# Five transpose groups per head pair, one-column row sums and turned keys in a two-block transformer kernel

## The reference, cut to what matters

```python
mod_l = jax.nn.silu(c) @ w_mod[l] + b_mod[l]          # modulation: rows of 512 columns at a time in the kernel
k = blockdiag(x_c, w_kblk)                            # mLSTM keys; the kernel wants them in both layouts
...
def one_block(qi):                                    # later layers, 128 queries at a time
    sc = jnp.einsum('bqkgd,bskd->bkgqs', qi, k_all, preferred_element_type=jnp.float32)
    p = jax.nn.softmax(sc, axis=-1).astype(v_all.dtype)
    return jnp.einsum('bkgqs,bskd->bqkgd', p, v_all)
```

## Time and profile before

| what | value |
|---|---|
| median of 3 runs | 3628.36 us (3626.59 to 3631.72) |
| the profiled execution | 3626.34 us |
| span of its instructions | 3624.6 us |
| mean granted TensorE clock | 0.948 |
| PE busy | 3266.9 us, 90% of the span |
| PEld busy | 2622.5 us, 72% |
| DVE busy | 1872.3 us, 52% |
| ACT busy | 1415.7 us, 39% |
| POOL busy | 694.9 us, 19% |

### The profile page before, as it was taken

One profiled execution on the slowest core, in us unless ns is written; L12 is line 12 of the kernel. 1 busy time (PEld: TensorE's weight loads), 2 busy tenths in 40 slices (PEclk: granted clock), 3 DMA queues, 4 the chain that ended last, 5 costly groups with the idle time before them and its releaser, 6 DMA issues. The chain is left out here.

```text
span 3624.6 us, 43080 instructions
## 1 busy us (share of the span) xinstructions
PE 3266.9 (90%) x17137; PEld 2622.5 (72%) x17137; DVE 1872.3 (52%) x2593; ACT 1415.7 (39%) x1941; POOL 694.9 (19%) x460
## 2 busy tenths in 40 slices
PE   7989998999999799794999999599988896998879
PEld 3767775778777687673788887588877675886757
DVE  4356775444444344646788888424415443152543
ACT  4222232333333244431777777431126334212640
POOL 2100001011111155300454554320010003000000
PEclk7999999999999899896999999799989997999999
DMA  6326555101000131324999999411121134112112
GB/s 197 113 96 199 168 173 175 33 25 43 26 25 25 50 116 64 129 88 166 350 382 390 379 389 374 137 60 54 38 60 24 47 111 156 57 44 57 30 70 82
DMA packets 248690, 471.51 MB, mean 130 GB/s; under 512 B 25455, under 2 KB 137072, under 8 KB 248492
## 3 DMA queue, kind: packets, MB, share of 16 engines
q1 hardware_dynamic: 232904, 410.88, 32.7%
q0 software_dynamic: 15264, 57.70, 4.8%
q10 hardware_dynamic: 324, 0.15, 0.0%
HBM read 406.12 MB, written 55.22 MB: 127 GB/s over the span
## 5 line engine op out<-in xcount | busy, mean ns | idle before, releaser
L2525 DVE TENSOR_TENSOR exp_wl<-wts_raw,exp_wh 128x2048 fp32r<-128x2048 f32 x144 | 393.9, 2771 | 106.2 <-ACT exp_wh L2485 106.2
L2485 ACT ACTIVATE exp_wh<-wts_raw 128x2048 fp32r<-128x2048 f32 x192 | 368.4, 1921 | 196.1 <-PE exp_gate L2414 64.1
L2691 PE MATMUL pr_ps<-l_h_high,pr_wh 128*128 128x512 f32 (+1 forms) x896 | 335.5, 374 | 0.0
L2692 PE MATMUL pr_ps<-l_h_low,pr_wh 128*128 128x512 f32 (+1 forms) x896 | 329.9, 368 | 0.0
L2693 PE MATMUL pr_ps<-l_h_high,pr_wl 128*128 128x512 f32 (+1 forms) x896 | 329.2, 367 | 0.0
L2384 POOL TENSOR_TENSOR exp_wl<-wts_raw,exp_wh 128x2048 fp32r<-128x2048 f32 x48 | 229.1, 4773 | 265.2 <-ACT exp_wh L2485 265.2
L842 PE MATMUL in_ps<-iw_h_high,in_wh 128*128 128x512 f32 (+1 forms) x696 | 273.2, 393 | 0.0
L843 PE MATMUL in_ps<-iw_h_low,in_wh 128*128 128x512 f32 (+1 forms) x696 | 263.4, 378 | 0.0
L844 PE MATMUL in_ps<-iw_h_high,in_wl 128*128 128x512 f32 (+1 forms) x696 | 263.0, 378 | 0.0
L2853 DVE TENSOR_TENSOR pr_wl<-pw_raw,pr_wh 128x512 fp32r<-128x512 f32 x84 | 57.8, 692 | 334.2 <-ACT pr_wh L2771 332.9
L2691 PEld LDWEIGHTS pr_ps<-l_h_high,pr_wh 128*128 128x128 f32 x896 | 170.3, 190 | 30.5 <-issue 2.4
(11 more groups left out here) (510 smaller groups left out, 7343.5 us busy)
## 6 DMA issues: line engine op xcount, KB each, us to landing
wts_raw<-in_w_e_gate SPq DMA_DIRECT2D x64, 1024.0 KB, 9.6
wts_raw<-in_w_e_up SPq DMA_DIRECT2D x64, 1024.0 KB, 8.8
wts_raw<-in_w_e_down SPq DMA_DIRECT2D x64, 1024.0 KB, 7.6
g_scratch<-in_w_mod SPq DMA_DIRECT2D x80, 512.0 KB, 4.5
pw_raw<-in_w_in SPq DMA_DIRECT2D x88, 256.0 KB, 2.9
iw_raw<-in_w_in SPq DMA_DIRECT2D x74, 256.0 KB, 4.6
mod_w<-in_w_mod SPq DMA_DIRECT2D x4, 2048.0 KB, 11.9
wo_w<-in_w_out SPq DMA_DIRECT2D x2, 4096.0 KB, 13.3
```

What stands on the lines that cost most here:

```text
L2485: act.activation(wh[:, m % RING], raw[:, m % RAW_RING], ACT.Copy).then_inc(high, 1)
L2525: dve.tensor_tensor(wl[:, m % RING], raw[:, m % RAW_RING], wh[:, m % RING].bitcast(F32), ALU.subtract).then_inc(low, 1)
L2691: nc.tensor.matmul(out, wh[:, slot, k, :], hi, start=h == 0 and k == 0, stop=False)
L2692: nc.tensor.matmul(out, wh[:, slot, k, :], lw, start=False, stop=False)
```

## The change

In `mod_rows` the table is replaced by one column of ones. A block's sums are made by four matmuls whose outputs are single rows at PSUM partitions 0, 32, 64 and 96, each over a part of the columns: a quarter of 512 where there is one vector, half of 512 of each where there are two. ACT copies 128 rows of 128 or 256 columns, and each of the two DMAs of a block sends four pieces or two.

In `mlstm` the eight latent token tiles of `k` are made by transposing `kT` in place of multiplying again; the use with the two context tiles stays a multiplication.

In `attention_2` a long pair has five groups of four transposes: `e0`, `e1` (tiles 0 to 7 of the even head), `tails` (the last two tiles of both heads), `o0`, `o1` (tiles 0 to 7 of the odd head). Scores of the next pair stand behind `e0` and `o0`. The value products of the pair before stand at the end of a pair, in bank 1, with no transposes beside them. DVE copies `o0`, ACT the other four; one reciprocal serves both heads; `leave` opens a pair's list on DVE. A short pair has `tails` alone.

```diff
@@ project_first, mod_rows and row
-                    accumulate(nc, ex[:], [(g.pick[:, 32 * (1 - s):32 * (1 - s) + P], accs[n % 3][:, s, :]) for s in MOD_BLOCKS[n][2]]).then_inc(
-                        ex_full, 1)
+                    for i, s in enumerate(conds):
+                        for h in range(parts):
+                            row = 32 * (i * parts + h)
+                            mm = nc.tensor.matmul(ex[row:row + 1, 0:wide], g.ones[:, 0:1], accs[n % 3][:, s, h * wide:(h + 1) * wide],
+                                                  start=True, stop=True, skip_group_check=True)
+                    mm.then_inc(ex_full, 1)
...
-                    act.activation(mrow[:], ex[0:64, :], ACT.Copy).then_inc(ex_act, 1)
+                    act.activation(mrow[:, 0:wide], ex[:, 0:wide], ACT.Copy).then_inc(ex_act, 1)
...
@@ mlstm, projections and project
+                            if q == 1 and c >= CT:
+                                parts.append((a * DH + t * P, P, kT[:, t, (c + a - CT) * P:(c + a - CT + 1) * P]))
+                                continue
...
+                            mm = pe.transpose(pb[:, use % 2, at:at + w], pairs, g.ident[:])
...
@@ attention_2
+        pieces = lambda u: ("e0", "e1", "tails", "o0", "o1") if long[u] else ("tails",)
+        bank = {"e0": 0, "e1": 1, "tails": 0, "o0": 1, "o1": 0, "out": 1}
...
+                    for what in pieces(u)[-3:]:
+                        await_left(pe, (u, what))
+                    await_left(pe, f, 1)
+                    pe.wait_ge(inv_ready, u + 1)
...
+                for u in range(len(units)):
+                    ahead = u + 1 < len(units)
+                    for what in pieces(u):
+                        turn_p(u, what)
+                        if ahead and what == pieces(u)[0]:
+                            scores(2 * u + 2)
+                        if ahead and what in ("o0", pieces(u)[0] if not long[u] else ""):
+                            scores(2 * u + 3)
+                    if u:
+                        output(u - 1)
+                output(len(units) - 1)
...
+                exp(0)
+                exp(1)
+                for u in range(len(units)):
+                    if long[u]:
+                        copy_four(u, "e0")
+                        copy_four(u, "e1")
+                    copy_tails(u)
+                    if u + 1 < len(units):
+                        exp(2 * u + 2)
+                    if long[u]:
+                        copy_four(u, "o1")
+                    if u + 1 < len(units):
+                        exp(2 * u + 3)
...
+                for u in range(len(units)):
+                    if u > 1:
+                        leave(u - 2)
+                    dve.wait_ge(exped, 2 * u + 2)
+                    n = 2 * u
+                    dve.reciprocal(inv[:, n % 8:n % 8 + 2], total[:, n % 4:n % 4 + 2]).then_inc(inv_ready, 1)
+                    if u + 1 < len(units):
+                        maximum(n + 2)
+                    if long[u]:
+                        copy_odd(u)
+                    if u + 1 < len(units):
+                        maximum(n + 3)
```

More of the change, by code:

```diff
@@ L1831, in project @@
                     for at, w, pairs in USE[use][1]:
-                        mm = accumulate(nc, pb[:, use % 2, at:at + w], pairs)
+                        if isinstance(pairs, list):
+                            mm = accumulate(nc, pb[:, use % 2, at:at + w], pairs)
+                        else:
+                            mm = pe.transpose(pb[:, use % 2, at:at + w], pairs, g.ident[:])
                     mm.then_inc(full[use % 2], 1)
@@ L3034, in attention_2 @@
         per_group = len(items) // KVH
-        groups = lambda keys: [(a, min(4, keys // P - a)) for a in range(0, keys // P, 4)]
-        V_USES = 3
-        first_use = [V_USES + sum(len(groups(k)) for _, _, k in items[:n]) for n in range(len(items) + 1)]
+        long = [keys > 4 * P for _, _, keys in units]
+        pieces = lambda u: ("e0", "e1", "tails", "o0", "o1") if long[u] else ("tails",)
+        bank = {"e0": 0, "e1": 1, "tails": 0, "o0": 1, "o1": 0, "out": 1}
+        fills = [("v", b) for b in range(2)] + [("v", 2)]
+        for u in range(len(units)):
+            fills += [(u, what) for what in pieces(u)] + ([(u - 1, "out")] if u else [])
+        fills.append((len(units) - 1, "out"))
+        bank_of = {f: f[1] % 2 if f[0] == "v" else bank[f[1]] for f in fills}
+        nth = {f: sum(bank_of[e] == bank_of[f] for e in fills[:n + 1]) for n, f in enumerate(fills)}
         lo = N_CTX if last else 0
@@ L3042, in side_of, with await_full, await_left @@
             return slice((n % 2) * HD, (n % 2) * HD + HD)
[L3044 to L3050, removed]
+        def await_full(eng, f):
+            eng.wait_ge(full[bank_of[f]], nth[f])
+        def await_left(eng, f, n=0):
+            if nth[f] > n:
+                eng.wait_ge(free[bank_of[f]], nth[f] - n)
         with nc.Block() as block:
@@ L3140, in scores @@
                     mm.then_inc(scored, 1)
-                for c, (t0, tn) in enumerate(groups(N_ALL)):
-                    turn(c, [g.parts[:, V_AT, (t0 + k) * P:(t0 + k + 1) * P] for k in range(tn)])
+                for c in range(3):
+                    turn(("v", c), [g.parts[:, V_AT, t * P:(t + 1) * P] for t in range(4 * c, min(4 * c + 4, NT))])
                 scores(0)
                 scores(1)
[L3146 to L3160, removed]
+                for u in range(len(units)):
[9 more added lines that the diff above has]
+                output(len(units) - 1)
             @block.scalar
@@ L3167, in exp @@
                     if n >= 2:
[L3168 to L3172, removed]
+                        await_full(act, ((n - 2) // 2, "o1" if n % 2 and long[(n - 2) // 2] else "tails"))
                     act.activation(p[:, n % 2, 0:keys], sc[:, n % 2].rearrange("p b n -> p (b n)")[:, 0:keys], ACT.Exp,
@@ L3227, in _ @@
                 maximum(0)
-                for n in range(len(items)):
-                    if n + 1 < len(items):
-                        maximum(n + 1)
-                    dve.wait_ge(exped, n + 1)
-                    dve.reciprocal(inv[:, n % 8:n % 8 + 1], total[:, n % 4:n % 4 + 1]).then_inc(inv_ready, 1)
-                    if n:
-                        copy_last(n - 1)
-                copy_last(len(items) - 1)
-                end = first_use[-1]
-                dve.wait_ge(full[end % 2], end // 2 + 1)
-                leave(end % 2, len(units) - 1).then_inc(y_scaled, 1)
+                maximum(1)
+                for u in range(len(units)):
+                    if u > 1:
[9 more added lines that the diff above has]
+                        maximum(n + 3)
+                leave(len(units) - 2)
+                leave(len(units) - 1)
 def back(ap, n):
```

91 lines of the change are left out of this document (52 added, 39 removed).

## The result

| | before | after |
|---|---|---|
| median of 4 runs each | 3627.48 us (3621.3 to 3631.72) | 3579.3 us (3577.7 to 3581.97) |
| the profiled execution, its span | 3626.34, 3624.6 us | 3581.97, 3580.2 us |
| mean granted TensorE clock | 0.948 | 0.947 |

The ratio of after to before is 0.9868, with a 95% interval of 0.9856 to 0.988: 48 us faster by the medians, 44.4 by the two profiled spans. The forecast was 3583, in a range of 3572 to 3604.

A forecast was written before the change was run, and what follows sets the result against it. PE's list was taken to bound project_first, the order of the lists the later attentions. Row sums 13, keys 4 and attention 28 us make 45: 3626.3 - 45 = 3581.3, 3583 for the median, range 3572 to 3604.

The forecast's parts named there:

- What bounds the kernel: PE's list sets project_first; mlstm's short matmuls need the timeline; in the later attentions the order of the lists counts.
- Row sums, the blocks: project_first: four matmuls run at once, saving 0.32 us in each of 10 blocks and 0.95 in 10 others, 12.7 us.
- One end of the range: Row sums in project_first: 18 us saved if switching the tiling mode costs nothing.
- Row sums, the end of the phase: ACT's last copy, DMA, copy in project_first: some 0.7 us shorter, with the DMA wait unchanged at 2.27 us.
- Keys: mlstm: transposed key tiles save 1.15 us in three heads and about 0.5 in the first, 4 us (0 to 4.6).
- Attention: Later attentions: 30 long pairs save 0.8 us each, 4 short pairs 1 us each, 28 us (0 to 33).
- The layout: One steady long attention pair scheduled by hand from measured durations: 7.8 us for 8.60, one stall of 0.55 before `o0`.
- One-column sums that don't run at once: project_first: row-sum matmuls run one after another, +6.6 us in place of -13, 3603 us; chance 0.08.
- DVE as the bound of project_first: DVE limits project_first, so only 5 of the 13 us are got, 3591 us; chance 0.08.
- Keys that lower the clock, for a stretch or to the end of a head: mlstm: transposes lower the clock; for a stretch 3589 us, chance 0.10; to each head's end about 3663, chance 0.02.
- The pair that stays at 8.6: Attention: a loop through DVE binds if the maximum ends over 1.2 us late; no gain, 3611 us; chance 0.07.
- The sum: Whole kernel: 13 + 4 + 28 = 45 us saved from the profiled 3626.3 us.

The follow-up runs named there:

- e1: Not a run: in a long attention pair, the second group of four transposes, of the even head's tiles 0 to 7; it has no measured time or ratio of its own.
- the whole sums: Kernel after with each row sum as one one-column matmul of 512 columns per vector, instead of pieces in different partition groups: 3588.95 us, ratio 0.9896.
- the keys alone: Kernel before with only the latent key tiles in mlstm made by transposing `kT`: 3621.93 us, ratio 0.9987.
- the odd kernel: Kernel after with the odd head's maximum taken twice on DVE in 29 long pairs: 3588.99 us, ratio 0.9889.

## Why the prediction held, step by step

- **What bounds the kernel** held: PE's list in all three phases. DVE's wait for the high parts in project_first went from 66.0 us to 55.9 in 325 us: it lost 10 of its slack to the 12 that PE gained, and is far from the bound.
- **Row sums, the blocks**: 12.7 us forecast; the stretch up to the last two blocks lost 12.4. From the third block to the last but one, clear of the phase's start, 6 blocks at 0.32 and 10 at 0.95 make 11.4 us, and 11.87 were measured. The saving a block, 0.35 and 0.95, and the switching cost, about 0.3, were those that `gates` gave. One end of the range was mis-added: without a switching cost it is 12.7 + 20 x 0.33 = 19.3, not 18.
- **Row sums, the end of the phase** was wrong, in sign: -0.7 forecast, +0.9 measured. Two terms were mis-sized. I put the landing at "the same 2.27 us (0 to 1 more)"; it was 1.04 more, the upper end, and with POOL's transfer held back the wait was 2.20. And I costed the issue of DMAs in four pieces at nothing; it takes 0.5 us more for a pair. The first pair's issue lies inside the wait, the second's behind the last copy, where it adds 0.48. 1.04 + 0.48, less 0.31 for each of two copies, is 0.9.
- **Keys**: 3.6 us from use 15 to `update` forecast, 3.58 measured, 1.2 less than before. The phase gained 4.6, the far end of the range, for the 4 that I took: the mis-sized term is the first head. I held POOL's `qw` to cap it at 0.5, but the main loop starts behind `update`'s first burst of matmuls, 3 us after `qw` had ended, so that head gained 1.2 like the others.
- **Attention**: 28 forecast, 27.4 measured. The layout's starts held within 0.1 us, the pair 7.8 against 7.76. The stall is 0.49 us by the starts (0.34 idle in the row) for 0.55. The count of pairs was off: between products 7.75 us stand 23 times in the two layers, not 30, and 23 x 0.85 make 19.6. The other 7.8 us came from the long pairs at the ends of a group, the short pairs and the passages between, for 7 x 0.8 + 4 = 9.6 in the forecast. That this part came out within 0.6 us is in part luck: the steady pairs gave 1.2 us more than 23 x 0.8, the others 1.8 less.
- **The rivals.** One-column sums that don't run at once: refuted by the whole sums. DVE as the bound of project_first: refuted by its 56 us of waits. Keys that lower the clock, for a stretch or to the end of a head: 1.00 in the stretch of the turned keys, 0.99 over the phase, with the keys alone too. (The stretch from 60 to 90 us of the earlier trace rows holds 72 transposes and, at its end, 6 matmuls of the projection, so it was not transposes alone.) The Trainium skill, "TensorE: Matmul & The Clock Gate", Part 4, says that the full clock doesn't engage for transposes; here 2.6 us of them with matmuls before and behind ran at full clock, so the measurement decides against a loss in this place. The pair that stays at 8.6: refuted, and its decision point was wrong as well. I put it at a maximum 1.2 us later than laid out; in the odd kernel the small operation behind it starts 1.4 us later (2713.32 - 2710.20 = 3.12 us behind the start of `o1`, in the kernel after 2732.57 - 2730.84 = 1.73), and the pair still takes 7.75.
- **The sum**: 45 forecast, 44.4 between the profiled spans. The sums gave 12.4 - 0.9 = 11.5 us for 13, the keys 4.6 for 4, the attention 27.4 for 28: 43.5 together. The remaining 0.9 is unchanged code, which scatters by more than that (2555.3 to 2561.3 in the table). So the mechanisms held, but that the total is off by only 0.6 us is in part luck: what the phase's end and the attention fell short by was made up by the keys and by that scatter.

## What to carry to other kernels

An order written out by hand can be costed by laying out one period from measured durations, bank by bank and engine by engine; it gave the starts within 0.1 us, and the one stall that it leaves says which piece of work to put there next (here another 0.46 us a pair). In this kernel one-column sums were worth their switching cost only where a vector's pieces, or several vectors, went to different groups of partitions at once. Where a small DMA is waited for, price its issue by its pieces and look at which large transfer on another queue goes out in the same microsecond.

## What the runs showed of the hardware beyond expectation

- Cutting a 2 KB row into pieces doubles the time to issue it on ACT's queue: two DMAs took 0.53 us with one piece each, 0.95 with two, 1.04 with four.
- A 512 KB transfer on POOL's queue held up a pair of 2 KB DMAs in four pieces each on ACT's by 1.1 us (a wait of 3.31 us, 2.20 without it).
- A second one-column matmul of 512 columns, into another group of 32 partitions, cost 0.01 us (27.94 for 27.93 between two blocks).
- 1.5 us of work on DVE in each pair left the steady period at 7.75 us: the copy that it delayed held up `tails` inside the gap in which PE waited for the copy of `e1` anyway.
